# Sample tile first: another order of the five token tiles through w_o, the norm and the routing of a one-core decoder step

## The chip, the core and the metric

The program runs on one core of a Trainium2 chip, in float32. Its time is the device time in microseconds (us) of one execution. The engines are named as in the profile: PE (TensorE, matmuls) and PEld (its weight loads), DVE (VectorE), ACT (ScalarE), POOL (GpSimd), and SP (SyncE), which here only issues DMAs. PEclk is the clock granted to TensorE: 1.00 is 2.4 GHz, 0.50 is 1.2 GHz.

## What is computed

One layer of a decoder for 512 prompt tokens and 64 sample tokens (8 requests of 8 tokens each), width 1024. This is the part that matters here:

```python
def trunk_layer(x, c, ...):
    ...
    merged = g_a * (y_a @ w_pa) + g_b * (y_b @ w_pb) + g_c * (y_c @ w_pc)
    x = layer_norm(ALPHA * x + (1 + g1) * (merged @ w_o), ln1_g, ln1_b)
    h2 = x * (1 + sc2) + sh2
    x = layer_norm(ALPHA * x + (1 + g2) * moe(h2, w_router, router_bias, w_e_gate, w_e_up, w_e_down), ln2_g, ln2_b)

def moe(h, w_router, router_bias, w_e_gate, w_e_up, w_e_down):
    scores = jax.nn.sigmoid(h @ w_router)             # 16 experts in 4 groups
    sel = scores + router_bias
    ...                                               # the best group, and the best two experts in it
    for e in range(N_EXPERTS):
        he = jax.nn.silu(h @ w_e_gate[e]) * (h @ w_e_up[e])
        y = y + gate[..., e:e + 1] * (he @ w_e_down[e])
```

Prompt tokens share one row of g1, sc2 and sh2; every sample request has rows of its own.

## The kernel before

The program has three stages: the projections and the three branches (up to about 617 us in the profiled execution), then **w_o, norm and routing** (617 to 714 us), which the change touches, and then the experts with the second norm.

In the middle stage the 576 tokens are five tiles. Tiles 0 to 3 hold 128 prompt tokens each, tile 4 holds the 64 sample tokens. `full_plan` lists the steps of the stage as keys, and PE, DVE, ACT and POOL each walk the same list and do their part of each key. All queues are in order, so the list is also the order on each engine:

- `("wo", t, h)`: PE multiplies tile t by half h of w_o (L2155; for the sample tile L2159, which puts the two column halves on two halves of the array). DVE then multiplies by g1, adds ALPHA * x from the buffer XR, and takes statistics (L1909 to L1918; for the sample tile L1912, L1914 in place of L1909). After half 1 it finishes the statistics, waits for POOL's rstd (L940) and writes h2 in two halves (L1925, L1928), each of which raises `h2_ready`.
- `("h2T", t, h)`: PE transposes half of h2 (L2125), ACT copies it out (L1335) and, after half 1, writes the normed x.
- `("rt", t)`: PE multiplies the transposed tile by w_router (L2121, 16 columns). ACT takes tanh (L1343), and DVE's `route` picks group and experts (L1570 to L1587) and raises `mask_ready`.
- `("cum", t)`: PE counts, for each token, the earlier tokens of each expert, with a triangular matrix and a matrix of ones (L2121). DVE's `near_rows` (L1593 to L1601) turns that into the places of the tokens that belong to the first expert tile.
- `("near", t)`: PE turns these places into a list of tokens (L2121); DVE adds it up over the tiles (L1948 to L1953). `("cnt",)` counts all tokens of each expert.

The first half of the k range of `("wo", t, 1)` is issued by PE just before `("rt", t - 1)`, so that it covers ACT's copy. After the last `near`, DVE raises `first_list`. POOL then gathers the first 128 rows of h2 from memory (L1030), where SP has stored every tile's h2 (L859, L864, signal `h2_out`); PE transposes them (L2522), and the experts begin (L2540 gate and up, L2549 flip, L2562 down). SP starts the stream of expert weights from the third expert on once that gather has landed.

Two buffers each of XR (x from memory), R and H2 alternate between tiles; XR is loaded by SP two tiles ahead (L850). While PE has nothing to do between steps of this stage it runs matmuls whose result nobody reads (`unread`, L2173), with the number set by the table `fillers`, and nine more before the gather lands.

## Time and profile before

| | |
|---|---|
| runs of the kernel before | 1037.85 us median of 3 (1037.19 to 1040.3) |
| profiled execution, device time | 1047.34 us |
| its span in the trace | 1045.5 us |
| PE busy | 1003.7 us, 96% of the span |
| DVE busy | 548.0 us, 52% |
| HBM read | 201.12 MB |
| chain that ended last | PE 86%, DVE 6%, DMA 3%, issue 3%, ACT 1% |

The profiled execution is slower than the median of the other runs by 9.5 us; all stretches below are of this one execution, in us from the start of its span. "Busy" of an engine counts its instructions, not its waits. In the trace a float32 matmul shows as two records of the same shape, so eight matmuls of 512 columns are 16 records.

### The profile page before, as it was taken

To read this page: it belongs to the slowest core of one execution; us is meant where nothing else is said; L and a number is where in the kernel's file an instruction comes from. 1 tells how busy PE (TensorE), PEld (TensorE's weight loads), DVE (VectorE), ACT (ScalarE), POOL (GpSimd) and SP (SyncE) were. 2 spreads that over 40 slices of the span, in tenths; PEclk is the share of its full clock that TensorE was granted. 3 is DMA by queue.
4 is the path that set the end of the run, shared out by engine and by line. 5 is a ranking of instruction groups with operands and counts; after the bars stand their busy time and mean duration, and the time that the engine had idled before them with its cause. 6 is when DMAs were issued, how large, how long until landed. Compare 5 with 4: busy or idle time off the path is not lost.

```text
span 1045.5 us, 23523 instructions
## 1 busy us (share of the span) xinstructions
PE 1003.7 (96%) x9535; PEld 722.8 (69%) x9535; DVE 548.0 (52%) x1381; ACT 198.9 (19%) x474; POOL 254.4 (24%) x284
## 2 busy tenths in 40 slices
PE   6999999999999999899999999999999999999995
PEld 5777777567776767567777764577876678667764
DVE  2122999983367888967446715587133121011137
ACT  2110112113232333232211100111111111111104
POOL 0100003634121223132435610001212122421123
PEclk9999999999999999999999999977999999999998
DMA  9964744644505215114081338243899999899995
GB/s 300 327 135 138 220 163 151 214 165 150 203 11 174 69 51 178 40 30 124 12 213 49 121 116 337 71 191 111 326 390 404 351 396 411 323 392 396 394 267 113
DMA packets 94003, 214.98 MB, mean 206 GB/s; under 512 B 23572, under 2 KB 48407, under 8 KB 89797
## 3 DMA queue, kind: packets, MB, share of 16 engines
q1 hardware_dynamic: 78388, 186.20, 50.0%
q0 software_dynamic: 6672, 19.67, 6.4%
q10 hardware_dynamic: 8841, 7.64, 2.6%
q8 instruction: 77, 1.26, 0.5%
q14 instruction: 25, 0.20, 0.1%
HBM read 201.12 MB, written 16.92 MB: 209 GB/s over the span
## 4 chain that ended last, share of the span: by engine, by line
PE 86%; DVE 6%; DMA 3%; issue 3%; ACT 1%; ACTq 0%; SPq 0%; POOL 0%; POOLq 0%; DVEq 0%
PE banks L2121 37%; PE banks L2540 15%; PE banks L2562 8%; PE banks L2135 6%; PE banks L2155 5%; PE banks L2125 3%; DMA arena<-in_w_ada 2%; PE banks L2243 1%; DMA arena<-expert_rows 1%; PE banks L2549 1%; PE banks L2522 1%; PE banks L2173 1%; PE banks L2371 1%; PE banks L2412 1%; DVE arena L1460 1%
## 5 line engine op out<-in xcount | busy, mean ns | idle before, releaser
L2121 PE MATMUL banks<-arena 128*128 128x288 f32 (+6 forms) x1774 | 427.9, 396 | 4.6 <-PE banks L2243 1.7
L2121 PEld LDWEIGHTS banks<-arena 128*128 128x128 f32 (+1 forms) x1774 | 318.0, 191 | 107.4 <-issue 30.2
L2540 PE MATMUL banks<-arena 128*32 128x256 f32 x3136 | 186.3, 380 | 1.8 <-issue 1.8
L2540 PEld LDWEIGHTS banks<-arena 128*32 128x32 f32 x3136 | 129.1, 109 | 47.3 <-issue 4.1
L2049 DVE TENSOR_TENSOR arena<-arena,banks 128x128 f32<-128x128 f32 x49 | 14.1, 288 | 220.0 <-ACT arena L1354 219.7
L2562 PE MATMUL banks<-arena 128*32 128x256 f32 x1568 | 101.8, 379 | 2.2 <-issue 1.9
L1052 POOL DMA_INDIRECT expert_rows<-arena,ints x44 | 43.0, 977 | 195.4 <-ACT arena L1365 191.3
L994 POOL TENSOR_SCALAR arena<-arena 128x288 f32<-128x288 f32 x46 | 45.4, 987 | 168.1 <-ACT arena L1276 101.8
L1431 DVE SCALAR_TENSOR_TENSOR arena<-arena 128x512 f32<-128x512 f32 x120 | 81.9, 742 | 0.0
L2562 PEld LDWEIGHTS banks<-arena 128*32 128x32 f32 x1568 | 61.4, 109 | 23.2 <-issue 6.7
L2135 PE MATMUL banks<-arena 128*128 128x288 f32 x256 | 65.1, 409 | 1.0 <-DVEq L1449 1.0
L2125 PE MATMUL banks<-arena 128*128 128x128 f32 (+7 forms) x295 | 45.7, 287 | 15.5 <-DMA arena<-constants 4.8
L2135 PEld LDWEIGHTS banks<-arena 128*128 128x128 f32 x256 | 47.3, 189 | 16.2 <-DVEq L1449 2.8
L2155 PE MATMUL banks<-arena 128*128 128x512 f32 x128 | 56.5, 594 | 1.1 <-DVE arena L1942 1.1
L2125 PEld LDWEIGHTS banks<-arena 128*128 128x128 f32 (+7 forms) x295 | 34.1, 150 | 29.5 <-issue 17.8
L1354 ACT ACTIVATE arena<-banks 128x128 f32<-128x128 f32 x49 | 13.6, 278 | 170.0 <-PE banks L2540 149.6
L2155 PEld LDWEIGHTS banks<-arena 128*128 128x128 f32 x128 | 23.7, 189 | 29.0 <-issue 29.0
L958 POOL TENSOR_TENSOR arena<-arena 9x512 f32<-9x512 f32 x8 | 13.2, 1652 | 122.7 <-ACTq L1171 122.7
L999 POOL TENSOR_TENSOR arena<-arena 128x288 f32<-128x288 f32 x30 | 28.6, 953 | 46.4 <-ACT arena L1283 39.0
L1490 DVE TENSOR_TENSOR arena<-arena 128x512 f32<-128x512 f32 (+3 forms) x48 | 36.6, 770 | 3.2 <-DVE arena L1534 0.7
L940 POOL TENSOR_TENSOR arena<-arena 128x1 f32<-128x1 f32 (+1 forms) x15 | 8.4, 561 | 114.5 <-DVE arena L1412 114.5
L1365 ACT ACTIVATE arena<-banks,arena 128x256 f32<-128x256 f32 x44 | 20.9, 475 | 73.0 <-PE banks L2562 73.0
(325 smaller groups left out, 1026.6 us busy)
## 6 DMA issues: line engine op xcount, KB each, us to landing
arena<-in_w_e_gate SPq DMA_DIRECT2D x16, 2048.0 KB
arena<-in_w_e_up SPq DMA_DIRECT2D x16, 2048.0 KB
arena<-in_w_e_down SPq DMA_DIRECT2D x16, 2048.0 KB
arena<-in_w_ada SPq DMA_DIRECT2D x8, 2048.0 KB, 9.7
arena<-in_w_in SPq DMA_DIRECT2D x8, 2048.0 KB, 9.8
arena<-in_w_ada SPq DMA_DIRECT2D x8, 1024.0 KB, 11.6
arena<-in_x_prompt SPq DMA_DIRECT2D x8, 512.0 KB, 7.2
arena<-in_w_in SPq DMA_DIRECT2D x14, 256.0 KB, 8.8
```

Of the source, the lines that this page charges most:

```text
L994: own.link(pool.tensor_scalar(GT[:, z, :], GT[:, z, :], 1.0, None, ALU.add))
L999: own.link(pool.tensor_tensor(PJ[:, z, :], GT[:, z, :], PJ[:, z, :], ALU.mult))
L1052: pool.indirect_dma_start(quarters, bass.IndirectOffsetOnAxis(ints[:, I_DEST + d:I_DEST + d + 1], 0), YR[:, yr_of(d), :], None).then_inc(s ...
L1365: act.activation(YR[:, yr_of(d), :], banks[6 + d % 2][:, 0:256], ACT.Copy, scale=WBLK[:, d:d + 1]).then_inc(ev("yo_up"), 1)
L1431: stt(ACC[:, j, 0:SEQ], arena[:, bass.ds(w + (A_AE + j * EXT), SEQ)], arena[:, bass.ds(w + (A_CK + j * CW), 1)], ACC[:, j, 0:SEQ], ALU.mul ...
L1490: tt_(out, a, b, op).then_inc(ev("summed"), 1)
L2121: last = pe.matmul(out, a, b, start=k == 0, stop=k == len(pairs_) - 1)
L2125: return pe.transpose(out, src, ident[0:src.shape[0], 0:src.shape[0]])
L2135: return pe.matmul(early_in(key).tile(key)[:, 0:HALF], a_rows[:, k, a:a + P], HT[:, k, h * HALF:h * HALF + HALF], start=k == 0, stop=k == ...
L2155: last = pe.matmul(ps, MG[:, k, t * P:t * P + P], w[k], start=k == 0, stop=k == KT - 1)
L2540: last = pe.matmul(out, HG[:, g % 2, k, a:a + BLK], both_weights(i, k, c), start=k == 0, stop=k == KT - 1)
L2562: last = pe.matmul(banks[6 + b % 2][BLK * c:BLK * c + BLK, 0:256], HETB[:, b % 2, k, :], w[:, k, 256 * c:256 * c + 256], start=k == 0, sto ...
```

## The change

The order of the tiles through the stage becomes a table, `TILE_AT = [4, 0, 1, 2, 3]`, and `NTH[t]` is a tile's place in it. The list of steps, the alternating buffers, SP's loads and stores and all counts of signals go by the place instead of the tile number. With the sample tile first, the counting of tokens is rewritten: every later tile adds the sample tile's mask (64 rows of ones) and the sum over earlier prompt tiles, so `cum` is up to three matmuls instead of two. The table of fillers changes too.

```diff
+TILE_AT = [4, 0, 1, 2, 3]
+NTH = {t: s for s, t in enumerate(TILE_AT)}
...
-    plan += [("wo", 4, 0), ("wo", 4, 1), ("near", 1), ("h2T", 3, 0), ("h2T", 3, 1), ("cum", 2), ("rt", 3), ("h2T", 4, 0), ("h2T", 4, 1), ("rt", 4)]
-    plan += [("cum", 3), ("near", 2), ("cum", 4), ("cnt",), ("near", 3), ("near", 4)]
+    tile = TILE_AT
+    for s in range(NT):
+        plan += [("wo", tile[s], 0)]
+        if s >= 2:
+            plan += [("cum", tile[s - 2])]
+        if s >= 3:
+            plan += [("near", tile[s - 3])]
+        if s:
+            plan += [("h2T", tile[s - 1], 0), ("h2T", tile[s - 1], 1), ("rt", tile[s - 1])]
+        plan += [("wo", tile[s], 1)]
+    plan += [("cum", tile[3]), ("near", tile[2]), ("h2T", tile[4], 0), ("h2T", tile[4], 1), ("near", tile[3]), ("rt", tile[4])]
+    plan += [("cum", tile[4]), ("cnt",), ("near", tile[4])]
...
+        def store_h2(s):
+            t = TILE_AT[s]
+            sp.wait_ge(ev("h2_ready"), 2 * s + 2)
+            sp.dma_start(h2_d[t * P:t * P + rows_of(t), :], H2[0:rows_of(t), s % 2, :]).then_inc(ev(f"h2_out{s % 2}"), 16)
...
-        fillers = {("h2T", 4, 0): (3, 256), ("cum", 3): (1, 256), ("near", 3): (1, 256)}
+        fillers = {("h2T", 3, 0): (4, 256), ("rt", 3): (1, 256), ("cum", 3): (3, 256), ("near", 3): (1, 256)}
...
-                last = mix_out(key, range(4 if key[1] in (1, 2, 3) and key[2] == 1 else 0, KT))
+                last = mix_out(key, range(4 if NTH[key[1]] > 0 and key[2] == 1 else 0, KT))
...
-                if t >= 2:
-                    pe.wait_ge(ev("sums_up"), t - 1)
-                so_far = [] if t == 0 else [(ones[:, 0:n], MSK[:, 0, :] if t == 1 else SUMM[:, t - 2, :])]
+                if s >= 3:
+                    pe.wait_ge(ev("sums_up"), s - 2)
+                so_far = [] if s == 0 else [(ones[0:NS, 0:n], MSK[0:NS, TILE_AT[0], :])]
+                if s >= 2:
+                    so_far += [(ones[:, 0:n], MSK[:, TILE_AT[1], :] if s == 2 else SUMM[:, s - 3, :])]
                 last = group(ps[0:n, 0:NE], so_far + [(tri[0:n, 0:n], MSK[0:n, t, :])])
```

The first place is PE at the start of the stage. Before, 24 matmuls of 512 columns (both halves of tile 0 and half 0 of tile 1) stand ahead of the first transposes (128x128):

```order
L2155 MATMUL banks<-arena 128x512 x24
L2125 MATMUL banks<-arena 128x128 x8
L2155 MATMUL banks<-arena 128x512 x4
L2121 MATMUL banks<-arena 128x16 x8
L2155 MATMUL banks<-arena 128x512 x12
```

Now the sample tile's 32 matmuls of 256 columns (two at a time on halves of the array) and eight of tile 0 stand ahead of the sample tile's transposes (128x64):

```order
L2170 MATMUL banks<-arena 64x256 x32
L2166 MATMUL banks<-arena 128x512 x8
L2136 MATMUL banks<-arena 128x64 x8
L2166 MATMUL banks<-arena 128x512 x4
L2132 MATMUL banks<-arena 64x16 x8
L2166 MATMUL banks<-arena 128x512 x12
```

Between the first tile's last w_o matmul and its transposes stand 8 matmuls of 512 columns, as before; what moved is that the first tile is the one of 64 tokens.

The second place is PE behind the last w_o matmuls. Before, the last rows with 32 matmuls are the sample tile's; its transposes (128x64) and router matmuls (64x16) come behind those of tile 3 (the last `cum`, `cnt` and `near` follow behind these rows):

```order
L2159 MATMUL banks<-arena 64x256 x32
L2121 MATMUL banks<-arena 128x1 x2
L2125 MATMUL banks<-arena 128x128 x8
L2121 MATMUL banks<-arena 128x16 x10
L2173 MATMUL banks<-arena 128x256 x3
L2125 MATMUL banks<-arena 128x64 x8
L2121 MATMUL banks<-arena 64x16 x8
L2173 MATMUL banks<-arena 128x256
L2121 MATMUL banks<-arena 128x16 x2
L2121 MATMUL banks<-arena 128x1 x2
```

Now the last w_o matmuls are tile 3's, and what follows (L2184 are the fillers) is:

```order
L2166 MATMUL banks<-arena 128x512 x4
L2132 MATMUL banks<-arena 128x16 x3
L2132 MATMUL banks<-arena 128x1 x2
L2184 MATMUL banks<-arena 128x256 x4
L2136 MATMUL banks<-arena 128x128 x8
L2132 MATMUL banks<-arena 128x1 x2
L2184 MATMUL banks<-arena 128x256
L2132 MATMUL banks<-arena 128x16 x8
L2184 MATMUL banks<-arena 128x256 x3
L2132 MATMUL banks<-arena 128x16 x5
L2184 MATMUL banks<-arena 128x256
L2132 MATMUL banks<-arena 128x1 x2
```

Only one tile's transposes and router matmuls are left behind the last w_o matmul, but of 128 tokens, and `("near", 2)` and a filler (rows 6 and 7) stand between its transposes and its router matmuls.

The third place is SP at the end of the stage. Before, the last store of h2 (64 rows) stands behind two loads of expert weights of 2 MB each:

```order
L859 DMA h<-arena 128x1024
L752 DMA arena<-in_w_e_down 128x4x1024
L760 DMA arena<-in_w_e_gate 128x4096
L864 DMA h<-arena 64x1024
```

The last store is now 128 rows, in the same place:

```order
L854 DMA h<-arena 128x1024
L757 DMA arena<-in_w_e_down 128x4x1024
L765 DMA arena<-in_w_e_gate 128x4096
L854 DMA h<-arena 128x1024
```

## Rows read from the trace of the kernel before

**Rows 1.** Windows, expert stage: length, busy of PE, PEld, DVE, ACT, POOL, PEclk, DMA share, GB/s.
```profile
860.00:900.00 40.00, 36.59 (x635) 29.06 (x631) 5.27 (x15) 5.11 (x13) 13.72 (x14) 1.00 0.99 398
```

**Rows 2.** Timeline of PE, 617 to 738 us: start, length, line, shapes, records, idle before.
```profile
617.33 20.88 PE L2155 MATMUL banks<-arena 128*128 128x512 f32 x48 [1.14 <-DVE arena L1942]
638.05 1.03 PE L2125 MATMUL banks<-arena 128*128 128x128 f32 x8
...
654.61 1.07 PE L2125 MATMUL banks<-arena 128*128 128x128 f32 x8
...
681.54 3.68 PE L2159 MATMUL banks<-arena 128*64 128x256 f32 x32
685.64 3.68 PE L2159 MATMUL banks<-arena 128*64 128x256 f32 x32 [0.42 <-PE banks L2159]
...
691.96 2.49 PE L2121 MATMUL banks<-arena 128*128 128x16 f32 x16 [0.48 <-ACT arena L1335]
...
698.81 1.86 PE L2121 MATMUL banks<-arena 128*64 128x16 f32 x16 [0.57 <-ACT arena L1335]
...
707.98 6.92 PE L2173 MATMUL banks<-arena 128*128 128x256 f32 x18
714.74 1.05 PE L2522 MATMUL banks<-arena 128*128 128x128 f32 x8
...
726.97 5.33 PE L2540 MATMUL banks<-arena 128*32 128x256 f32 x64
...
737.26 3.66 PE L2540 MATMUL banks<-arena 128*32 128x256 f32 x64
```

**Rows 3.** Timeline of DVE in the stage, same columns.
```profile
626.59 0.69 DVE L1909 TENSOR_TENSOR arena<-banks,arena 128x512 f32<-128x512 f32 x1 [1.75 <-DMA arena<-in_x_prompt]
...
681.65 0.69 DVE L1909 TENSOR_TENSOR arena<-banks,arena 128x512 f32<-128x512 f32 x1 [0.55 <-PE banks L2155]
...
686.29 1.42 DVE L1928 SCALAR_TENSOR_TENSOR arena<-arena 128x512 f32<-128x512 f32 x2
...
687.87 0.42 DVE L1912 TENSOR_TENSOR arena<-banks,arena 64x256 f32<-64x256 f32 x1
...
694.99 1.41 DVE L1928 SCALAR_TENSOR_TENSOR arena<-arena 64x512 f32<-64x512 f32 x2
...
700.99 0.17 DVE L1570 TENSOR_SCALAR arena<-arena 64x16 f32<-64x16 f32 x1 [0.23 <-ACT arena L1343]
...
703.49 0.17 DVE L1593 COPY arena<-banks 128x16 f32<-128x16 f32 x1
...
704.28 0.43 DVE L1601 TENSOR_TENSOR arena<-arena 128x256 f32<-128x256 f32 x1
...
708.28 0.15 DVE L1953 CAST ints<-arena 128x1 int32<-128x1 f32 x1
```

**Rows 4.** Windows of 2 us around the changes of PE's clock, columns as in rows 1.
```profile
692.00:694.00 2.00, 2.00 (x15) 2.00 (x15) 1.21 (x4) 0.95 (x1) 0.55 (x1) 0.79 1.03 410
712.00:714.00 2.00, 2.00 (x7) 1.64 (x6) 1.86 (x6) 0.00 (x0) 0.00 (x0) 0.59 0.19 76
728.00:730.00 2.00, 2.00 (x24) 1.03 (x20) 1.64 (x9) 0.00 (x0) 0.81 (x1) 0.50 0.00 0
```

**Rows 5.** Timeline of SP's queue of DMA issues.
```profile
616.31 0.38 SPq L637 DMA_DIRECT2D arena<-in_w_o  x1
...
689.44 0.40 SPq L752 DMA_DIRECT2D arena<-in_w_e_down  x1
...
696.42 0.54 SPq L864 DMA_DIRECT2D h<-arena  x1
```

**Rows 6.** DMA issues, 610 to 780 us: count, KB each, us from issue to landing.
```profile
arena<-in_w_o SPq DMA_DIRECT2D x1, 1024.0 KB, 5.3
arena<-in_x_sample SPq DMA_DIRECT2D x1, 256.0 KB, 3.9
h<-arena SPq DMA_DIRECT2D x1, 256.0 KB, 6.1
```

More of the change, by code:

```diff
@@ L280, in full_plan @@
         plan += g(7) + nxt(2) + q(7) + rows(2) + nxt(3) + g(4) + rows(3) + q(4) + rows(4)
-    for t in range(4):
-        plan += [("wo", t, 0)]
-        if t >= 2:
-            plan += [("cum", t - 2)]
-        if t >= 3:
-            plan += [("near", t - 3)]
-        if t:
-            plan += [("h2T", t - 1, 0), ("h2T", t - 1, 1), ("rt", t - 1)]
-        plan += [("wo", t, 1)]
-    plan += [("wo", 4, 0), ("wo", 4, 1), ("near", 1), ("h2T", 3, 0), ("h2T", 3, 1), ("cum", 2), ("rt", 3), ("h2T", 4, 0), ("h2T", 4, 1), ("rt", 4)]
-    plan += [("cum", 3), ("near", 2), ("cum", 4), ("cnt",), ("near", 3), ("near", 4)]
+    tile = TILE_AT
[10 more added lines that the diff above has]
+    plan += [("cum", tile[4]), ("cnt",), ("near", tile[4])]
     return plan
@@ L1331, in _ @@
                 act.wait_ge(*tt.full(key))
-                if t and h == 0:
-                    act.wait_ge(*at.full(("rt", t - 1)))
+                s = NTH[t]
+                if s and h == 0:
+                    act.wait_ge(*at.full(("rt", TILE_AT[s - 1])))
                 src = tt.tile(key).rearrange("p (k n) -> p k n", n=P)
@@ L1891, in _ @@
                 _, t, h = key
-                n = rows_of(t)
-                r, x = R[0:n, t % 2, :], XR[0:n, t % 2, :]
+                n, s = rows_of(t), NTH[t]
+                r, x = R[0:n, s % 2, :], XR[0:n, s % 2, :]
                 cols = slice(512 * h, 512 * h + 512)
                 pick = "p" if t < 4 else "s"
-                if h == 0 and t == 0:
+                if h == 0 and s == 0:
                     dve.wait_ge(ev("merged"), 48)
@@ L2169, in unread @@
         def unread(times, cols):
-            pe.wait_ge(*mm.taken(("wo", 3, 1)))
+            pe.wait_ge(*mm.taken(("wo", 2, 1)))
             for _ in range(times):
-                pe.matmul(mm.tile(("wo", 3, 1))[:, 0:cols], ident, con[:, 0:cols], start=True, stop=True)
-        fillers = {("h2T", 4, 0): (3, 256), ("cum", 3): (1, 256), ("near", 3): (1, 256)}
+                pe.matmul(mm.tile(("wo", 2, 1))[:, 0:cols], ident, con[:, 0:cols], start=True, stop=True)
+        fillers = {("h2T", 3, 0): (4, 256), ("rt", 3): (1, 256), ("cum", 3): (3, 256), ("near", 3): (1, 256)}
         pe.wait_ge(ev("consts"), 16)
@@ L2200, in _ @@
             split = kind in ("lg", "pt") and key[1] != "s"
-            if kind == "rt" and key[1] < 3:
-                mix_out(("wo", key[1] + 1, 1), range(0, 4))
+            if kind == "rt" and NTH[key[1]] < NT - 1:
+                mix_out(("wo", TILE_AT[NTH[key[1]] + 1], 1), range(0, 4))
             if not split and kind != "wo":
@@ L2484, in _ @@
                 n = rows_of(t)
-                pe.wait_ge(ev("near_hot"), t + 1)
-                last = group(ps[:, 0:1], [(HOT[0:n, t % 2, e, :], con[0:n, K_TOK + t:K_TOK + t + 1]) for e in range(2)])
+                s = NTH[t]
+                pe.wait_ge(ev("near_hot"), s + 1)
+                last = group(ps[:, 0:1], [(HOT[0:n, s % 2, e, :], con[0:n, K_TOK + t:K_TOK + t + 1]) for e in range(2)])
             if not split:
```

72 lines of the change are left out of this document (37 added, 35 removed).

## Prediction

> **What bounds the kernel.** I read the shares of the engines first: PE is busy for 96% of the span and the chain that ended last runs through it, so an edit counts by what it does to PE's waits, or to the moment at which the experts can begin. In the expert stage nothing hides a delay: PE is busy 36.59 of 40 us in its slackest stretch, while the DMA engines are busy 0.99 of the time, so PE and the weight stream run side by side [rows 1]. Both start from one event, the landing of the first gather of h2, and this hangs on the last tile's routing. So the question is when the first list is ready.
>
> Then the timelines of PE and DVE from 617 to 738 us. In the middle stage PE is gapless until 685 us. One round (transposes, half a tile of w_o, router, three quarters of a tile's w_o) takes 654.61 - 638.05 = 16.56 us [rows 2]. DVE has some slack in each round, but not at the end: tile 3's norm starts at 681.65, the sample tile's w_o is complete on PE at 685.64 + 3.68 = 689.3, yet DVE turns to the sample tile only at 687.87 and has its first half of h2 at 694.99 + 0.7 = 695.7 [rows 2, 3]. From there one routing follows another until the list is cast at 708.28 + 0.15 = 708.43 [rows 3]. From tile 3's last w_o matmul (681.54) that is 26.9 us; from the end of all w_o matmuls 19.1 us. PE meanwhile has little work, and its granted clock falls from 2.4 to 1.2 GHz between 692 and 694 (mean 0.79) and is back only in 712 to 714 (0.59), with a second fall around 728 to 730 [rows 4].
>
> **What the change removes at the end.** Behind the last w_o matmul stands one norm and one routing instead of nearly two. I add up the new tail from T0, the end of tile 3's w_o matmuls.
> - DVE starts 0.11 after T0 (681.54 to 681.65). The halves of h2 are ready after another 686.29 + 0.71 - 681.65 = 5.35 and 6.06; DVE is free after 687.87 - 681.65 = 6.22 [rows 2, 3].
> - Router matmuls of tile 3 now stand behind `near` of tile 2, and that waits for DVE's `near_rows` of tile 2, which comes after the norm: 704.28 + 0.43 - 703.49 = 1.22 [rows 3]. That is T0 + 7.55, about 0.3 to 1 us later than ACT's copy would let them start. With `near` itself and one filler (a 512-column record takes 20.88 / 48 = 0.435 at 2.4 GHz, so a filler of two 256-column records 0.44, or 0.87 at 1.2 GHz [rows 2]) and four small records (0.5, or up to 0.9; a router record takes 1.86 / 16 = 0.12 to 2.49 / 16 = 0.16 [rows 2]) the router starts at T0 + 8.6 at the high clock, T0 + 9.5 at the low one.
> - Router matmuls: tile 3's took 2.49 partly at the high clock, the sample tile's 1.86 at the low one with half the stationary columns [rows 2]. No row has 128 columns wholly at the low clock. Bounds: 2.49 and twice 1.86 = 3.7.
> - To `route` 700.99 - 700.67 = 0.32, `route` itself 703.49 - 700.99 = 2.5 [rows 2, 3]. `cum` with three matmuls instead of two, six records, 0.8 to 1.0; the one added matmul is 0.3 of it. `near_rows` 1.22. The last `near` and DVE's add and cast 1.0 to 1.4.
> - Sum: T0 + 16.9 at the high clock, T0 + 19.6 at the low clock.
>
> The fillers cost nothing in this sum except the one ahead of the router: the four stand in PE's wait for h2, the three in its wait for `route`.
>
> The Trainium skill bears on one term: in "TensorE: Matmul & The Clock Gate", section "LDWEIGHTS (loading the stationary operand)", a load costs by its columns, P / 1.2 ns. By that rule 16 loads of 128 instead of 64 columns cost about 0.85 us more than the sample tile's, 2.7 us in all, and the high-clock sum would be 0.2 us longer. The rows above stand between 2.49 and 3.7 and agree with its direction: it speaks against the change, since the tile that is now last has twice the columns.
>
> **What it adds before the end.** T0 moves. Three rounds and a half lay between the first transposes and tile 3's last w_o matmul (681.54 - 638.05 = 43.49 us); now there is one round more, 60.05 [rows 2]. When do the first transposes start? PE needs two times 685.64 - 681.54 = 4.10 for the sample tile and 20.88 / 3 = 6.96 for half of tile 0, and is there at 632.5 [rows 2]. The half of w_o that the second sample group needs is issued at 616.31 and takes 5.3, so it lands at 621.6, 0.2 late [rows 5, 6]. DVE, though, cannot start before x has landed. Before, that was at 626.6, after a wait of 1.75 for it [rows 3]. The sample tile's x is 256 KB less, 0.6 us at the 410 GB/s of a busy stretch [rows 4]; I take 0.4 less, 626.2 (bounds 626.0 and 626.6). The sample norm takes from 687.87 to 695.7, 7.8 us [rows 3], which gives 634.0. Before, x had been there for 4.6 us when PE finished tile 0 at 617.33 + 2 x 6.96 = 631.2, and only half of the chain was left; now both halves of the first tile wait for x, behind the same cover of 6.96 us. So PE waits 1.3 to 1.9 us, and 0.3 more between the two halves. T0 = 634.0 + 0.4 + 60.05 = 694.4. What lies behind this wait is all of the stage, since PE has no slack in it.
>
> **Sum.** First list at 694.4 + 16.9 = 711.3 up to 694.4 + 19.6 = 714.0, against 708.43: +2.9 to +5.6 us. I take +4.0, as the clock, which before fell 3 to 4 us after the last w_o matmul, should fall during the new tail too (between T0 + 4 and T0 + 8), so the early steps run high and the late ones low. Behind the list the chain is as before: nine fillers (6.92, mostly at the low clock [rows 2]) cover the gather, and the transposes at 714.74 and the experts move by the same 4.0. The other loads of x and stores of h2 keep their place in the rounds, two tiles ahead, and stay hidden under a round of 16.56. Against the profiled execution's own 1047.34 this gives 1051.3; the median of the runs is 9.5 lower, and I put the same difference on it: 1037.85 + 4.0 = 1041.9 us.
>
> **Rivals.**
> - *The first wait does not come* (x of the sample tile lands early). Alone, such a load lands 3.9 us after its issue [rows 6]. Then DVE follows PE, the sample h2 is there at about 631, before 632.5, and 1.8 us are saved: +2.2 (1 to 3.5). Against it: it is issued at the same point behind the same w_o, router and constants loads as before, and the first x took until 626.6.
> - *The clock holds, and the change is not slower.* Nine fillers stand in the tail instead of five. If the clock stays at 2.4 GHz from T0 until the experts, the tail is its lower bound, +2.9; the nine fillers before the gather end in 4 us instead of 6.92 and PE takes the gather up when it lands, at best 0.7 sooner; and the second fall, which cost 5.33 - 3.66 = 1.7 in one block [rows 2], goes too: +0.5, and -1.3 with the first rival's saving. It decides from the point at which PE's work between T0 and T0 + 12 suffices to keep the clock. Against it: four fillers last 1.75 of the 5.4 us in which PE waits for h2, and before, much denser work between 689 and 692 did not hold it [rows 4].
> - *The low clock reaches into the experts.* If it comes back 5 us later than before, relative to the list, the fillers (18 records of 0.435 at twice the time, 7.8) and the first two blocks (3.66 each [rows 2]) stretch: +3 to +4 on top, +7.5 in all.
> - *The last h2 store is late.* It is twice as long and stands behind 4 MB of weights, now issued at T0 instead of 689.44; before it landed 6.1 after 696.42, at 702.5 [rows 5, 6]. 4.2 MB at 410 GB/s are 10.2 us and start some 1.5 us after the issue: 706.1, then 1.3 and about 0.6 for landing, 708.0. The gather waits for it only if the list is ready before that, and then by up to 1 us. It is hidden unless the tail is 3 us shorter than I think.
> - *Nothing shows*, because PE waits in the expert stage (3.4 us in 860 to 900 [rows 1]) take a delay up. The weight stream starts from the same gather and moves with it, so I give this little: 0 to +1.5.
>
> The Trainium skill has a sentence on the second rival: "TensorE: Matmul & The Clock Gate", Part 4 on transposes, says that transposes do not count as busy PE in the way matmuls do. By it tile 3's transposes would not help to hold the clock, and the rival would hang on the fillers alone. In the trace the fall at 692 to 694 comes just after transposes and router matmuls, which fits.
>
> **Numbers.** About 0.3% (3.1 us) is what a measurement of this kernel can tell from no change. Likeliest case, +2.9 to +5.6 (1040.7 to 1043.5): 0.45. First wait absent: 0.15. Clock holds: 0.18. Low clock into the experts: 0.10. Nothing shows or the store decides: 0.12. Slower by over 3.1: most of the first case (0.40) and the fourth (0.10), 0.50. Faster by over 3.1: half of the clock rival, if more falls of the clock vanish than I counted, 0.09. The rest, 0.41, is no difference. The range leaves out the far ends of the second and third rivals: 1036.0 to 1044.8.
>
> **What would show it.** In the new trace: PE idle of 1.3 to 2.2 us before the first transposes at 632 to 634; tile 3's last w_o matmul ending near 694.4; its router matmuls starting 8.6 to 9.5 later, behind `near` and not behind ACT; the list cast 16.9 to 19.6 after T0; PEclk 0.50 in most of 702 to 714; the gather's transposes near 718.7. The prediction is wrong if PE has no wait at 632 and the clock stays at 1.00, or if T0 comes more than 1 us from 694.4, since then a round is not what I take it for.

## The result

Timed on one chip against the kernel before, the changed kernel takes 1049.39 us (median of 4 runs, 1048.0 to 1051.23), the kernel before 1038.88 (4 runs, 1037.19 to 1040.3). The ratio is 1.0098, 95% interval 1.0073 to 1.0124, so **+10.2 us** (the two medians are 10.5 apart) where I had forecast +4.0. The direction was right; the time lies outside the range. The profiled execution of the changed kernel took 1051.23 us with a span of 1049.4.

The two profiled spans can't be compared. From the first expert block to the second norm before took 299.1 us, after 289.6, and this difference is not the change's. In the table of the experiments it goes by session, for both orders alike: 289.5 to 290.2 in some sessions, 296.4 to 299.7 in the others, and never both in one session. The median of the kernel before goes with it, 1038.3 to 1040.6 us in the former and 1046.2 to 1049.5 in the latter. One chip has had both. I found no cause; a ratio within one session is free of it, a difference of times between sessions is not. So below I read the middle stage by itself: from the first w_o matmul to the transposes of the gathered rows (L2522 before, L2539 after). It took 714.74 - 617.33 = 97.4 us [rows 2] and now takes 727.73 - 618.95 = 108.8. That is +11.4, enough for the whole loss. (The stage starts 1.6 us later in this execution; later executions of both kernels start anywhere from 617 to 622.)

The timeline of PE after has start, length, line, shapes, records and idle before them. L2170 is the sample tile's w_o, L2166 a prompt tile's, L2136 the transposes, L2132 router, counting and lists:

```profile
618.95 3.68 PE L2170 MATMUL banks<-arena 128*64 128x256 f32 x32 [1.14 <-DVE arena L1953]
623.38 3.68 PE L2170 MATMUL banks<-arena 128*64 128x256 f32 x32 [0.75 <-DMA arena<-in_w_o]
...
636.59 0.43 PE L2136 MATMUL banks<-arena 64*128 64x64 f32 x4 [2.46 <-DVE arena L1939]
637.25 0.66 PE L2136 MATMUL banks<-arena 64*128 64x64 f32 x4 [0.23 <-DVE arena L1939]
637.84 6.67 PE L2166 MATMUL banks<-arena 128*128 128x512 f32 x8
...
698.17 3.69 PE L2166 MATMUL banks<-arena 128*128 128x512 f32 x8
```

PE waits 0.75 us for w_o, and the first transposes stand behind another wait of 2.46 for DVE. Then compare rows that are the same amount of work: the eight records of w_o behind the transposes take 6.67 us at 637.84, in before the same eight took 3.60 (a row of before further down), and eight later ones take 3.69 here (698.17). The cause is TensorE's clock, as windows of 2 us show (PEclk is the number ahead of the last two):

```profile
634.00:636.00 2.00, 0.13 (x1) 0.00 (x0) 1.58 (x2) 0.00 (x0) 0.27 (x1) 1.00 0.96 410
...
638.00:640.00 2.00, 2.00 (x3) 0.97 (x4) 1.38 (x2) 1.46 (x2) 0.00 (x0) 0.50 1.01 406
...
644.00:646.00 2.00, 2.00 (x19) 1.30 (x18) 0.15 (x1) 0.18 (x1) 0.00 (x0) 1.00 0.97 401
```

It is 1.00 in 634 to 636, where PE waits, 0.50 (1.2 GHz) from 638, just behind the wait, and back at 1.00 from 644. The next three fences are: DVE's row, which tells what it waited for; the list of DMA issues, which tells how long the load took (KB, us from issue to landing); and DVE again, with the copy of tile 3's count and the cast of the list:

```profile
628.48 0.42 DVE L1923 TENSOR_TENSOR arena<-banks,arena 64x256 f32<-64x256 f32 x1 [5.47 <-DMA arena<-in_x_sample]
```
```profile
arena<-in_x_sample SPq DMA_DIRECT2D x1, 256.0 KB, 8.0
```
```profile
719.23 0.17 DVE L1603 COPY arena<-banks 128x16 f32<-128x16 f32 x1 [1.47 <-PE banks L2132]
...
722.17 0.15 DVE L1964 CAST ints<-arena 128x1 int32<-128x1 f32 x1
```

The sample tile's x, 256 KB, takes 8.0 us from issue to landing, where before it took 3.9 as the last load of its kind [rows 6]. The tail behind the last w_o matmul, which ends at 698.17 + 3.69 = 701.86 (T0):

```profile
707.43 1.29 PE L2136 MATMUL banks<-arena 128*128 128x128 f32 x8 [2.09 <-DVE arena L1939]
709.48 0.98 PE L2132 MATMUL banks<-arena 128*128 128x1 f32 x4 [0.76 <-DVE arena L1612]
...
711.32 3.43 PE L2132 MATMUL banks<-arena 128*128 128x16 f32 x16
...
717.65 2.50 PE L2132 MATMUL banks<-arena 64*128 64x16 f32 x10 [0.16 <-issue]
...
727.73 1.05 PE L2539 MATMUL banks<-arena 128*128 128x128 f32 x8
```

The router matmuls (711.32) stand behind `near` (709.48), which waits for DVE's L1612, the end of `near_rows`: as forecast. The clock is 1.00 up to 708, 0.67 in 708 to 710, 0.50 to 724, so these sixteen records take 3.43 us against 1.85 at the high clock (655.02 in x_first, below). The list is cast at 722.17 + 0.15, T0 + 20.5. Tile 3's h2 store (512 KB), issued at 707.97, took 10.5 us in the list of DMA issues from 700 us on. It landed at 718.5, 3.8 us ahead of the list, so it is hidden.

### The profile page after: what moved, and what is told of

Its sections match the earlier page's. It is cut to its first block and busy times, and to the rows that moved or that the text cites. A ratio compares the mean times of both kernels' runs of the same rounds, so it can differ in the third digit from the quotient of the medians.

```text
span 1049.4 us, 23552 instructions
## 1 busy us (share of the span) xinstructions
PE 1002.5 (96%) x9549; PEld 695.0 (66%) x9549; DVE 548.3 (52%) x1381; ACT 199.2 (19%) x474; POOL 253.7 (24%) x284
## 5 line engine op out<-in xcount | busy, mean ns | idle before, releaser
L2132 PE MATMUL banks<-arena 128*128 128x288 f32 (+7 forms) x1780 | 429.1, 396 | 4.4 <-PE banks L2254 1.7
L2132 PEld LDWEIGHTS banks<-arena 128*128 128x128 f32 (+2 forms) x1780 | 318.5, 191 | 110.8 <-issue 33.8
L2557 PE MATMUL banks<-arena 128*32 128x256 f32 x3136 | 178.7, 377 | 2.0 <-issue 2.0
L2557 PEld LDWEIGHTS banks<-arena 128*32 128x32 f32 x3136 | 105.8, 108 | 66.0 <-issue 2.1
L2579 PE MATMUL banks<-arena 128*32 128x256 f32 x1568 | 94.8, 381 | 0.0
L2579 PEld LDWEIGHTS banks<-arena 128*32 128x32 f32 x1568 | 51.7, 110 | 24.9 <-issue 1.0
L2136 PE MATMUL banks<-arena 128*128 128x128 f32 (+7 forms) x295 | 46.1, 289 | 21.2 <-DMA arena<-constants 5.7
L2166 PE MATMUL banks<-arena 128*128 128x512 f32 x128 | 60.0, 621 | 0.0
L2136 PEld LDWEIGHTS banks<-arena 128*128 128x128 f32 (+7 forms) x295 | 34.0, 149 | 35.6 <-issue 23.0
L2166 PEld LDWEIGHTS banks<-arena 128*128 128x128 f32 x128 | 24.6, 198 | 28.7 <-issue 28.5
L1363 ACT ACTIVATE arena<-banks 128x128 f32<-128x128 f32 x49 | 13.6, 278 | 155.1 <-PE banks L2557 155.1
## 6 DMA issues: line engine op xcount, KB each, us to landing
arena<-in_w_e_down SPq DMA_DIRECT2D x16, 2048.0 KB, 17.4
arena<-in_w_ada SPq DMA_DIRECT2D x8, 1024.0 KB, 11.4
```

Of the source, the lines that this page charges most:

```text
L2132: last = pe.matmul(out, a, b, start=k == 0, stop=k == len(pairs_) - 1)
L2136: return pe.transpose(out, src, ident[0:src.shape[0], 0:src.shape[0]])
L2166: last = pe.matmul(ps, MG[:, k, t * P:t * P + P], w[k], start=k == 0, stop=k == KT - 1)
L2557: last = pe.matmul(out, HG[:, g % 2, k, a:a + BLK], both_weights(i, k, c), start=k == 0, stop=k == KT - 1)
L2579: last = pe.matmul(banks[6 + b % 2][BLK * c:BLK * c + BLK, 0:256], HETB[:, b % 2, k, :], w[:, k, 256 * c:256 * c + 256], start=k == 0, sto ...
```

## The experiments

They ran in five sessions; each ratio is against before in the same session (R is the session of the result; that of before's own profile is not on record). The stages, in us, are those of one profiled execution of each. T0, the end of the last w_o matmul, is counted from the first one; the tail goes from T0 to the transposes of the gathered rows; "experts" goes from the first expert block to the second norm. A run with no interval was timed once.

| kernel | session | order | time, ratio (interval) | T0 | tail | stage | experts |
|---|---|---|---|---|---|---|---|
| before | - | old | - | 72.0 | 25.4 | 97.4 | 299.1 |
| before_again | 1 | old | 1046.6 (before 1046.2) | 72.0 | 24.1 | 96.1 | 296.4 |
| after | R | new | 1.0098 (1.0073 to 1.0124) | 82.9 | 25.9 | 108.8 | 289.6 |
| changed_again | 2 | new | 1.0084 (1.0056 to 1.0112) | 81.2 | 23.6 | 104.8 | 297.6 |
| changed_third | 4 | new | 1055.8 (before 1049.5) | 80.9 | 24.7 | 105.6 | 297.1 |
| x_first | 1 | new | 1.0071 (1.0047 to 1.0095) | 76.7 | 25.8 | 102.6 | 297.5 |
| clock_kept | 1 | new | 1.0083 (1.0057 to 1.0109) | 79.3 | 25.9 | 105.2 | 299.5 |
| sample_second | 1 | 0, 4, 1, 2, 3 | 1.0061 (1.0038 to 1.0084) | 80.3 | 24.7 | 105.0 | 299.7 |
| count_folded | 2 | new | 1054.6 (before 1047.6) | 76.3 | 25.8 | 102.1 | 297.6 |
| list_late | 2 | new | 1049.3 (before 1047.6) | 77.2 | 23.8 | 100.9 | 297.6 |
| tail_filled | 3 | new | 1.0055 (1.0033 to 1.0077) | 77.2 | 23.9 | 101.1 | 289.8 |
| all_together | 2 | new | 0.9999 (0.9984 to 1.0014) | 76.4 | 22.1 | 98.5 | 297.6 |
| count_late | 3 | new | 1.0009 (0.9988 to 1.0030) | 75.4 | 22.4 | 97.7 | 290.2 |
| before_filled | 3 | old | 1.0011 (0.9986 to 1.0035) | 72.0 | 25.9 | 97.8 | 289.5 |
| old_late_x | 3 | old | 1.0026 (1.0004 to 1.0047) | 75.4 | 24.2 | 99.5 | 289.7 |
| old_late_again | 4 | old | 1055.5 (before 1049.5) | 78.3 | 24.2 | 102.6 | 299.5 |
| old_late_third | 5 | old | 1045.8 (before 1040.6) | 77.7 | 24.5 | 102.1 | 289.6 |
| old_later_x | 4 | old | 1060.8 (before 1049.5) | 84.2 | 24.6 | 108.8 | 297.6 |
| old_less_late | 5 | old | 1041.4 (before 1040.6) | 73.5 | 24.9 | 98.4 | 290.1 |

In the expectations "to the last w_o matmul" is counted to the start of its last record, 0.4 to 0.6 us ahead of the T0 of this table, and the tail from there. The letters of the theories are those that the expectations give them. before_again is the kernel before in one more execution: its middle stage is 96.1 us, so 97.4 was no accident.

**x_first.** SP issues the sample tile's x ahead of the loads of w_router, the constants and the bias, directly behind w_o.

```diff
+        load_x(0)
         sp.dma_start(WRT, I["w_router"]...).then_inc(ev("router_in"), 16)
...
-            sp.dma_start(XR[0:rows_of(t), s % 2, :], src).then_inc(ev(f"xr_in{s % 2}"), 16)
+            if s >= 1:
+                load_x(s)
```

> The changed kernel, with the load of the first tile's x issued ahead of the loads of w_router, the constants and the bias, 1.5 us earlier. Theory A: of the loss of about 10 us, 3.4 are PE's waits at the start for x (2.46 and 0.23) and for w_o (0.75), and 3.1 the fall of the clock that follows (8 records of w_o in 6.67 us instead of 3.6). Then x lands near 7 us after the first w_o matmul instead of 9.5, the wait shrinks to about 1, and the clock may hold: 1.5 to 4.6 us faster than the changed kernel, 1045 to 1048. Rival B (all of the loss is in the tail behind the last w_o matmul, since PE's time before it is made good by waits that vanish later): no change, 1049.

The timelines of DVE and PE (L2141 transposes, L2171 a prompt tile's w_o, L2137 small matmuls):

```profile
625.19 0.42 DVE L1928 TENSOR_TENSOR arena<-banks,arena 64x256 f32<-64x256 f32 x1 [1.53 <-DMA arena<-in_x_sample]
```
```profile
634.60 0.71 PE L2141 MATMUL banks<-arena 64*128 64x64 f32 x8
635.24 3.71 PE L2171 MATMUL banks<-arena 128*128 128x512 f32 x8
638.88 1.10 PE L2137 MATMUL banks<-arena 128*64 128x16 f32 x16
...
650.43 0.28 PE L2137 MATMUL banks<-arena 64*64 64x16 f32 x2
650.65 1.09 PE L2141 MATMUL banks<-arena 128*128 128x128 f32 x8
...
655.02 1.85 PE L2137 MATMUL banks<-arena 128*128 128x16 f32 x16
...
667.22 1.25 PE L2137 MATMUL banks<-arena 64*128 64x16 f32 x8
668.40 1.10 PE L2141 MATMUL banks<-arena 128*128 128x128 f32 x8
...
685.35 1.34 PE L2137 MATMUL banks<-arena 64*128 64x16 f32 x10 [0.30 <-PE banks L2171]
686.55 1.07 PE L2141 MATMUL banks<-arena 128*128 128x128 f32 x8
...
692.61 3.69 PE L2171 MATMUL banks<-arena 128*128 128x512 f32 x8
```

x lands 5.6 us after the first w_o matmul instead of 9.5, the transposes have no idle ahead of them, and the half tile behind them takes 3.71 us: no wait, no fall. T0 is 76.7 instead of 80.9 to 82.9. So the late load and what followed from it cost 4 to 6 us of T0. By the times the gain is smaller, 1.0071 against 1.0084 and 1.0098, with intervals that overlap; the traces, not the times, carry this reading.

**clock_kept.** The x stays late; five unread matmuls stand in PE's wait for it.

```diff
+            if key == ("h2T", TILE_AT[0], 0):
+                pe.wait_ge(*mm.room(("wo", TILE_AT[1], 1)))
+                for _ in range(5):
+                    pe.matmul(mm.tile(("wo", TILE_AT[1], 1))[:, 0:256], ident, con[:, 0:256], start=True, stop=True)
```

> The changed kernel, with five more unread matmuls of 256 columns ahead of the first transposes, in the wait for the sample tile's h2. The wait stays, the idle goes. Theory A: the clock does not fall at 637 us and the 3.1 us come back, 1046.3. If the clock falls all the same, or if its fall cost nothing that the end sees (rival B): 1049.

```profile
632.78 2.32 PE L2200 MATMUL banks<-arena 128*128 128x256 f32 x10
...
635.96 3.71 PE L2166 MATMUL banks<-arena 128*128 128x512 f32 x8
```

The five (L2200) take 2.32 us, just the wait, and the half tile of w_o takes 3.71 us instead of 6.67. T0 is 3.6 us sooner than in the first profile of the changed kernel and 1.6 to 1.9 sooner than in the two others. The half tile is 3.0 of the 3.6, and 1.6 to 1.7 of the others: that is the fall of the clock by itself. The time (1.0083) does not show it: its interval holds both the changed kernel's ratio and the forecast gain.

**sample_second.** The order is 0, 4, 1, 2, 3, so that the stage starts with a prompt tile, as in before.

```diff
-TILE_AT = [4, 0, 1, 2, 3]
+TILE_AT = [0, 4, 1, 2, 3]
...
```

> The changed kernel with the order 0, 4, 1, 2, 3: a prompt tile is first, the sample tile second; the end of the stage stays as in the changed kernel. Theory A: the start is as in the kernel before, no wait of PE for x and no fall of the clock there, so 6.5 us come back: 1043. Rival B: 1049, since the end is the same. Theory C (the sample tile's short matmuls and its counting, now ahead of the last w_o matmul, cost PE more than their 11 us wherever they stand): in between, 1045 to 1047, with rounds still longer than before's 16.6 us.

```profile
638.60 1.29 PE L2136 MATMUL banks<-arena 128*128 128x128 f32 x8 [2.13 <-DVE arena L1939]
639.82 3.41 PE L2170 MATMUL banks<-arena 128*64 128x256 f32 x16
```

The wait came back at another place: between tile 0's w_o and its transposes stands half a tile of 64 tokens, 3.68 us of work in place of 7, so PE waits 2.13 us for tile 0's h2, with x long there, and the clock falls behind it (3.41 us for 16 records of the sample tile, where 32 take 3.68 at 2.4 GHz [rows 2]). That the start would be as in before was my miss. So x early is not enough: what needs cover is the 7 to 8 us of a norm on DVE.

**changed_again** and **changed_third.** The changed kernel in two more executions.

> The changed kernel, unchanged, on the chip of this call. Its stage (first w_o matmul to the transposes of the first gather) was 108.7 us in its trace, against 97.4 and 96.1 in two traces of the kernel before; the kernel with the early x load had 102.5. If the stage is what sets the loss, it takes 108 to 109 again and the ratio to the kernel before is 1.010 to 1.011 (11 to 12 us), above that of the kernel with the early x load (1.007). If the loss comes from the expert stage or from the chip, the stage stays and the ratio is another.

> The changed kernel in a third execution. In the first its half tile of w_o behind the wait took 6.67 us, in the second 5.30 us, against 3.60. Theory F (chance): a third length, anywhere from 3.60 to 7.2 us, so 79 to 82.5 us from the first to the last w_o matmul. Rival G (the new order's wait always brings the clock down, because of what lies ahead of it): over 5 us again, 80.5 to 82.5 us.

```profile
636.33 0.43 PE L2136 MATMUL banks<-arena 64*128 64x64 f32 x4 [2.14 <-DVE arena L1939]
...
637.40 5.30 PE L2166 MATMUL banks<-arena 128*128 128x512 f32 x8
```
```profile
636.65 0.43 PE L2136 MATMUL banks<-arena 64*128 64x64 f32 x4 [1.87 <-DVE arena L1939]
...
637.67 5.40 PE L2166 MATMUL banks<-arena 128*128 128x512 f32 x8
```

The wait (2.14 and 1.87 us) and a fall behind it are there each time, but the fall costs 1.7 and 1.8 us where it cost 3.1 in the first: with that and other stretches of low clock in the tail the stage is 3 to 4 us shorter than in the first profile, where I had expected 108 to 109 again. So of the +11.4 of that profile some 3 belong to that execution.

**count_folded.** On top of x_first: the sample tile's mask is added into the running sum on DVE, so that each count is two matmuls again, not three.

```diff
-                so_far = [] if s == 0 else [(ones[0:NS, 0:n], MSK[0:NS, TILE_AT[0], :])]
-                if s >= 2:
-                    so_far += [(ones[:, 0:n], MSK[:, TILE_AT[1], :] if s == 2 else SUMM[:, s - 3, :])]
+                so_far = [] if s == 0 else [(ones[:, 0:n], GATE[:, 0, :] if s == 1 else SUMM[:, s - 2, :])]
...
```

> The kernel with the early x load, and the sample tile's mask, padded with zeros to 128 rows, is added by DVE into the running sum, so that a count is two matmuls again, all of them over 128 rows. Theory D: the third matmul and the change between matmuls over 64 and over 128 rows cost PE what the rounds are longer by: 1.25 and 1.34 + 0.30 us for the counting, against 0.95 and 0.9 before, in all about 1 us before the last w_o matmul, and some 0.5 in the tail. Stage 101.0 instead of 102.5. If the counting is hidden, 102.5.

T0 moved by 0.4 us where I had expected 1, the tail not at all where I had expected 0.5. The third matmul is cheap. That the rest of the cost is the counting itself is what count_late tests below.

**list_late** and **tail_filled.** Both on top of x_first. The first puts the list of tile 2 behind tile 3's router matmuls; the second leaves that order and doubles the unread matmuls in the tail's waits.

```diff
-... ("h2T", tile[4], 1), ("near", tile[3]), ("rt", tile[4])]
+... ("h2T", tile[4], 1), ("rt", tile[4]), ("near", tile[3])]
```
```diff
-        fillers = {("h2T", 3, 0): (4, 256), ("rt", 3): (1, 256), ("cum", 3): (3, 256), ("near", 3): (1, 256)}
+        fillers = {("h2T", 3, 0): (8, 256), ("rt", 3): (2, 256), ("cum", 3): (3, 256), ("near", 3): (1, 256)}
```

> The kernel with the early x load, with the list step of tile 2 moved behind the router matmuls of tile 3. In the changed kernel these start 2.6 us after the last transposes, as they stand behind the wait for DVE's places (0.76), the list step (0.85) and a filler (1.0), all at 1.2 GHz; ACT's copy would let them start about 1.2 us after. Theory E: 1.0 to 1.5 us less in the tail, stage 101.2. Rival: DVE's work is what the list waits for, and the list step now stands in the way later: stage 102.5 or more.

> As x_first, with more unread matmuls in the tail: eight instead of four in PE's wait for tile 3's h2 and two instead of one ahead of the router matmuls; counting and list as in the change. If the low clock is what made the tail of the changed kernel 26.4 us, these eight hold it at the high one through the router matmuls (1.85 instead of 3.43 us) and the tail is 23.5 to 24.5; stage 99.8 to 100.8 against 102.5, time 1.0045 to 1.005 of before. If the tail is set by the order near before rt and by DVE, 25.5 to 26.5 us and 1.0065 to 1.007.

```profile
702.76 2.77 PE L2137 MATMUL banks<-arena 128*128 128x16 f32 x20
```
```profile
704.82 1.85 PE L2137 MATMUL banks<-arena 128*128 128x16 f32 x16
```

In list_late the router starts 8.2 us after T0 instead of 9.46 and the 20 records take 2.77 us. In tail_filled eight unread matmuls (L2189) fill 3.7 us of the wait for h2, the clock holds to 710, and the router matmuls take 1.85 instead of 3.43. Each has a tail some 2.0 us shorter than x_first's, as forecast. But one profile each does not show that the edit did it. In changed_again, whose tail has the steps and the fillers of after, the clock held to 714 as well, and its router matmuls (L2132) took:

```profile
708.63 1.85 PE L2132 MATMUL banks<-arena 128*128 128x16 f32 x16
```

Its tail is 23.6 us without any edit, that of changed_third, with 3.43 us for these matmuls, 24.7. What an execution's clock does there is worth as much as either edit, and the times don't settle it: list_late was timed once, and the interval of tail_filled overlaps that of x_first. Whether more fillers hold the clock in this tail is not shown.

**all_together** has x first, the folded count, the late list and the filled tail; **count_late** also moves the count of tile 1 and the list of tile 0 behind T0.

```diff
-        if s >= 2:
+        if 2 <= s < NT - 1:
             plan += [("cum", tile[s - 2])]
-        if s >= 3:
+        if s == 3:
             plan += [("near", tile[s - 3])]
...
+    plan += [("cum", tile[2]), ("near", tile[1]), ("cum", tile[3]), ("h2T", tile[4], 0), ("h2T", tile[4], 1), ("rt", tile[4]), ("near", tile[2]), ("near", tile[3])]
```

> The sample tile first, with the early x load, the folded counting, the late list step and, against the fall of the clock in the tail, eight fillers instead of four before tile 3's transposes and two instead of one before its router matmuls. If all the causes named are right: stage 102.5 - 1.5 - 1.3 - 2 (router matmuls and counting at 2.4 GHz) = 97.7, level with the kernel before (ratio 1.000 to 1.003). If the order itself costs, because the last tile has 128 rows and nothing follows it that could cover its chain, 100 or more and a ratio above 1.004.

> As all_together (x first, folded counting, list behind the router), and the count of tile 1 and the list of tile 0, which PE did between w_o matmuls of tile 3 (a record group of 1.02 us and 0.30 us of idle), are moved behind the last w_o matmul, where PE waits for tile 3's norm; two of the eight unread matmuls there are taken out for it. If all that PE can put off gains where PE is the bound, the last w_o matmul ends 1.3 us sooner (74.4 us after the first instead of 75.7), and the tail of 22.7 us is unchanged, since DVE's added step of 1.2 us lies while PE transposes and multiplies by w_router: the time is 0.9985 to 0.9990 of before. Rival: DVE has two such steps between the norm and the routing (2 x 1.2 us), which then start later than ACT's result: the tail grows by 1 to 1.3 us and the time is 1.000.

```profile
705.93 2.36 PE L2141 MATMUL banks<-arena 128*128 128x16 f32 x20
```

Router and list together take 2.36 us at the high clock. These kernels remove the loss and gain nothing: 0.9999 and 1.0009, both intervals across 1 and below those of x_first and tail_filled. Their tails (22.1 and 22.4) are also below every tail of the changed order without these edits (23.6 to 25.9). So the edits of the tail do work together; the share of each stays open. The new order then has a tail 1.8 to 3.3 us shorter than the two profiles of before and a T0 3.4 to 4.4 us later. count_late brought T0 forward by 1.0 (expected: 1.3), so the counting does cost PE where it stood.

**before_filled.** The old order with more unread matmuls in its tail.

```diff
-        fillers = {("h2T", 4, 0): (3, 256), ("cum", 3): (1, 256), ("near", 3): (1, 256)}
+        fillers = {("rt", 3): (1, 256), ("h2T", 4, 0): (6, 256), ("rt", 4): (1, 256), ("cum", 3): (3, 256), ("near", 3): (2, 256)}
```

> The old order, with more unread matmuls in its tail: one ahead of tile 3's router matmuls, six instead of three ahead of the sample tile's transposes, one ahead of its router matmuls, three instead of one ahead of the last count and two instead of one ahead of the last list. If the low clock in the tail costs the old order what it seemed to cost the new one, and more work of PE holds it up, the tail (last w_o matmul to the gather's transposes) takes 22.5 to 23.5 us instead of 24.5 to 25.8, and the time is 0.998 of before. Rival: DVE's chain of two norms and two routings sets the tail and the clock stretches only PE's parts of it, some of which the added matmuls now delay: 24 to 26 us, 0.9995 to 1.001.

```profile
691.69 1.93 PE L2121 MATMUL banks<-arena 128*128 128x16 f32 x16
...
697.54 1.07 PE L2121 MATMUL banks<-arena 128*64 128x16 f32 x16
...
703.28 1.76 PE L2121 MATMUL banks<-arena 128*64 128x16 f32 x8 [1.88 <-issue]
```

The clock holds through both routers (1.93 and 1.07 us instead of 2.49 and 1.86 [rows 2]) and nothing is won: the last count starts at 703.28 behind 1.88 us of idle. It needs the mask that DVE's route ends with at 703.2, and DVE has no gap of over 0.25 us from 694.7 to there. Counted from the first w_o matmul that mask is ready at 86.1 us in both kernels, whatever PE's clock did; the list is cast 0.85 us later than before, as more fillers now stand ahead of the last list. The rival was right. In the old order the tail goes through DVE, so a faster PE gains nothing there.

**old_late_x, old_late_again, old_late_third, old_later_x, old_less_late.** The old order; tile 0's x is loaded behind weights of 2 MB and the x of tile 1 (three executions), behind 2 MB more, and behind 2 MB alone. They ask whether the wait and the fall belong to the new order.

```diff
         for t in range(NT):
+            if t == 0:
+                expert_weights(sp, 0, 0, 0)
+            for v in ([1, 0] if t == 0 else [] if t == 1 else [t]):
...
             if t == 1:
-                expert_weights(sp, 0, 0, 0)
```

> The old order of tiles; the x of tile 0 is loaded behind the x of tile 1 and behind the expert weights of 2 MB that stood behind both. Nothing else is changed. Before, tile 0's x landed at 626.6, 9.3 us after the first w_o matmul. Behind 2.5 MB at about 400 GB/s it lands some 6 us later, at 632 to 634. Theory A (a wait of PE of 2 us or more between dense stretches costs itself and, behind it, some 3 us at the low clock, whatever the order of tiles): the norm needs 7.8 us from there, so PE waits 2 to 3.5 us before its first transposes (at 638.05 before), and the clock falls behind the wait: the four w_o matmuls behind the transposes take 5 to 7 us instead of 3.60; from the first to the last w_o matmul 76 to 78 us instead of 71.6, the time 1.0045 to 1.006 of before. Rival (the fall belongs to the new order, whose short tile leaves PE with little work ahead of the wait): PE waits, but the half tile of w_o takes 3.6 to 3.7 us; 74 to 75 us, 1.0025 to 1.003.

> The kernel of old_late_x once more, for another execution. PE waits 2.85 us before its first transposes again. Theory F (chance: whether the clock falls behind a wait of two to three microseconds changes from one execution to the next): the half tile of w_o behind the transposes takes more than 4 us this time, with even odds, and the last w_o matmul ends 76 to 78 us after the first instead of 75.0. Rival G (the old order keeps the clock, whatever the execution): 3.61 us, and 75.0 again.

> The kernel of old_late_x a third time. PE waits 2.8 to 4.5 us before its first transposes. Theory F (chance, the same wait sometimes meets a fall): for a wait under 3 us even odds of a half tile of w_o of over 4 us behind it instead of 3.61. Theory H (in the old order a wait under 3 us is stood, a longer one not): 3.61 us if the wait is under 3, over 4 us if it is over 4.

> As old_late_x, with one more load of 2 MB ahead of tile 0's x, so that it lands some 4 to 5 us later still. PE waits 7 to 8 us before its first transposes instead of 2.85. If the length of the wait decides (theory H), the clock falls now, during or behind the wait: the half tile of w_o behind it takes 6 to 7.2 us instead of 3.61, and the last w_o matmul ends 82 to 84 us after the first. If the old order keeps the clock whatever the wait (rival G): 3.61 to 3.7 us, and 79 to 80 us.

> The old order, with tile 0's x behind one load of expert weights of 2 MB, but ahead of tile 1's x. It lands 1.3 us sooner than in old_late_x, so PE waits 1.5 to 2.2 us. Theory F: even odds of a fall, as the 1.87 us of changed_third had one. Theory H: no fall, 3.61 us for the half tile of w_o behind the transposes, last w_o matmul 73.3 to 74.3 us after the first.

```profile
644.50 1.29 PE L2127 MATMUL banks<-arena 128*128 128x128 f32 x8 [2.85 <-DVE arena L1930]
645.63 3.61 PE L2157 MATMUL banks<-arena 128*128 128x512 f32 x8
```
```profile
645.41 1.94 PE L2127 MATMUL banks<-arena 128*128 128x128 f32 x8 [4.41 <-DVE arena L1930]
647.15 4.41 PE L2157 MATMUL banks<-arena 128*128 128x512 f32 x8
```
```profile
644.09 1.75 PE L2127 MATMUL banks<-arena 128*128 128x128 f32 x8 [3.71 <-DVE arena L1930]
645.63 4.71 PE L2157 MATMUL banks<-arena 128*128 128x512 f32 x8
```
```profile
651.60 1.94 PE L2127 MATMUL banks<-arena 128*128 128x128 f32 x8 [9.46 <-DVE arena L1930]
653.33 5.17 PE L2157 MATMUL banks<-arena 128*128 128x512 f32 x8
```
```profile
641.87 1.29 PE L2127 MATMUL banks<-arena 128*128 128x128 f32 x8 [0.95 <-DVE arena L1930]
643.00 3.61 PE L2157 MATMUL banks<-arena 128*128 128x512 f32 x8
```

L2127 is the transposes, L2157 the half tile behind them. Waits of 4.41, 3.71 and 9.46 us are followed by a fall (4.41, 4.71 and 5.17 us for 3.6 us of work, and transposes of up to 1.94 instead of 1.03); 0.95 and 2.85 us are not. In the longest wait the clock is down to 0.50 already in 648 to 650, while PE still waits. So wait and fall come in the old order too once its first load is late. What the new order does for certain is to leave less work ahead of the first transposes, which makes the wait. For waits of 2 to 3 us the cases disagree: falls behind 1.87, 2.13, 2.14 and 2.46 in the new orders, none behind 2.85 in the old one. Chance (theory F) and something that the old order has ahead of its wait both stay possible, since no second wait under 3 us came in old_late_again and old_late_third. That is left open.

## Why the forecast was too small

- **Right.** The direction; the two waits at the start in kind, though both were longer than I had them (2.46 + 0.23 us for the sample tile's h2 against 1.3 to 1.9 + 0.3, and 0.75 for w_o's second half against 0.2); router matmuls at T0 + 9.46 (8.6 to 9.5), behind `near`; 3.43 us for them, between the bounds 2.49 and 3.7; a fall to 0.50 in the tail; h2's store hidden, though it landed 16.6 us after T0 instead of 13.6. None of the rivals "the first wait does not come", "the clock holds" and the low clock in the experts came true in this profile: the clock is back at 1.00 at 726, a second fall in the experts (a mean of 0.79 in 744 to 752) is there as it was before [rows 4].
- **T0 = 694.4, so 77.1 after the first w_o matmul, failed** by the test that I had set for it: it is 82.9. Three terms add up. The first transposes start 17.6 us after the first w_o matmul, not 16.7 (+1.0): I had x landing 8.9 us in, 0.4 sooner than before for its smaller size, and it took 9.5; and from there to the first half of h2 it was 636.59 - 628.48 = 8.1 us, not 7.8. The half tile behind the wait took 6.67 instead of 3.60 (+3.1), the largest of the three and a term that I had left out: I wrote of the clock in the tail only, and priced a wait by its length (clock_kept and x_first show it gone; in two other executions it is 1.7 and 1.8). And the rounds: I took one more round at 16.56 us. In x_first, where nothing disturbs them, they are 650.65 - 634.60 = 16.05, then 17.75, 18.15 and 696.30 - 686.55 = 9.75, in sum 61.7 instead of 60.05 (+1.65). The 16.56 was before's first round, with a count of two records. Its own second round, which I didn't look at, has a full count and a list, and takes 671.87 - 654.61 = 17.26; the added round is of that kind. That gives 0.7 of the 1.65. The other 0.95 is what is left of a first round 0.5 shorter (it has the sample tile's transposes and router), a second 0.5 longer and a third 0.9 longer, in which counts and lists take 1.18 and 1.50 us of PE in place of 0.80. (Between the first transposes and tile 3's last w_o matmul lay two full rounds and 9.67 us, not the "three rounds and a half" of the prediction; its sum adds one round, as it must.) PE in before (L2121 counts and lists):

```profile
638.92 3.60 PE L2155 MATMUL banks<-arena 128*128 128x512 f32 x8
...
654.47 0.29 PE L2121 MATMUL banks<-arena 128*128 128x16 f32 x2
...
671.07 0.95 PE L2121 MATMUL banks<-arena 128*128 128x16 f32 x8
671.87 1.07 PE L2125 MATMUL banks<-arena 128*128 128x128 f32 x8
```

- **T0 to the list, 16.9 to 19.6, was 20.5**, 2.5 over the 18.0 in the sum. The clock fell 6 to 8 us after T0, as I had it, and did not come back before 724, so every step of PE was at its slow end. Beyond my upper end it went by three steps: `cum` for tile 3 took 719.23 - 717.65 = 1.6 us up to DVE's copy instead of 0.8 to 1.0, `near_rows` 1.56 instead of 1.22, and the last `near` with add and cast 1.53 instead of 1.0 to 1.4. In the two other executions of the changed kernel the list is cast at 717.27 + 0.15 (changed_again) and 719.79 + 0.15 (changed_third), T0 + 17.4 and T0 + 19.5, both inside the forecast; the first has the clock at 1.00 until 714. From the list to the gathered rows' transposes it was 5.4 instead of 6.3 (-0.9).
- **The sum:** the forecast of 4.0, 5.8 for T0, 2.5 for the tail up to the list and -0.9 behind it make 11.4, which is what the stage shows. By the ratio it is 10.2, and in the other two profiles of the changed kernel the stage is 7.4 to 9.5 us longer than in those of before.
- **What the model itself lacked.** Even with wait, clock, list and count mended the order gains nothing. The reason is in T0: before ends it at 72.0, x_first at 76.7. Ahead of it now stand the sample tile's transposes and router matmuls (635.24 - 634.60 and 1.10, 1.7 us), which stood in the tail, where PE waited for DVE anyway. And counts and lists take 0.22 + 1.18 + 1.50 = 2.9 us of PE between w_o matmuls in x_first (650.43, 667.22, and 685.35 with its 0.30 of idle), against 0.14 + 0.80 = 0.94 in before (654.47, 671.07): one more count and one more list are pulled in front of T0. That is 3.7 of the 4.7; the other 1.0 I have not taken apart (PE's wait of 0.64 for w_o's second half is in it). So the tail got shorter, as DVE has one routing less in it, but PE work moved from where PE was idle to where it is the bound.

The rows bear on one rule used in the prediction. Router matmuls of a 128-token tile take 1.85 us at 2.4 GHz in x_first (655.02) and those of the sample tile 1.10 (638.88), 0.75 apart. "TensorE: Matmul & The Clock Gate" of the Trainium skill, section "LDWEIGHTS (loading the stationary operand)", gives the time of a load by its columns, from which I had estimated 0.85: the trace agrees within 0.1. At 1.2 GHz the rows are 3.43 and 1.86 [rows 2], 1.57 apart, so at the low clock the difference doubles. The prediction had added the 0.85 to the 1.86 of a low-clock row; its 2.7 us is neither the 1.85 nor the 3.43.

## What to carry to other kernels

When a step is moved ahead of the last big matmul, ask for each of its instructions whether PE was idle where it stood and is busy where it goes: a shorter dependent tail pays only for what it does not pull in front. The first item of a stage has its load exposed: look at what SP issues ahead of it, and give the chain behind it a cover as long as the chain. A wait of PE inside dense work can cost more than its length. Behind the 1.87 to 2.46 us of the changed kernel the low clock cost 1.7 to 3.1 us more, behind 2.85 us in the old order nothing, so look at the rows behind the wait. And before an edit is given the credit for a shorter stretch, look at what the clock does there in two executions of the kernel without it.

## What I had not expected of the hardware

- A load of 256 KB took 8.0 us to land behind w_router, constants and bias (64, 206 and 8 KB), and was there 5.6 us after the first w_o matmul, not 9.5, when issued directly behind w_o.
- Ahead of the last counts and lists between w_o matmuls PE shows 0.30 us of idle that no other engine releases (685.35 in x_first). No run here tells what it is.
- In three executions of the same kernel the fall of the clock behind the first wait cost 3.1, 1.7 and 1.8 us, and one wait of 2.85 us in the old order had none.
- The expert stage, which no edit touched, took 289.5 to 290.2 us in three sessions and 296.4 to 299.7 in the three others, for either order of tiles.
